# A two-layer hybrid encoder step: latent projections and their norm at head 0, norm crossings by pairs of tiles on the vector engine

## The reference

```python
h = rmsnorm(x, g_pre_mix)
(qn, qr, ckv, kr, qb, kb, vb, qc, kc, vc, alr, gc, gate) = split_cols(h @ w_in)
# A: latent attention, 8 heads: c = rmsnorm(ckv, g_kv); keys c @ w_uk, values c @ w_uv; rope on qr and kr
# B: sliding-window attention, 8 query heads on 2 key heads, window 128, sinks and ALiBi
# C: gated linear attention, 4 heads: loga = log_sigmoid(alr @ w_alpha + b_alpha) / 16,
#    a recurrence over tokens, then rmsnorm(o, g_gla) * silu(gc)
y = sigmoid(gate_a) * (oa @ w_up_a) + sigmoid(gate_b) * (ob @ w_up_b) + sigmoid(gate_c) * (oc @ w_up_c)
x = x + rmsnorm(y @ w_out, g_post_mix)
f = square(relu(rmsnorm(x, g_pre_mlp) @ w_ff1)) @ w_ff2          # d_ff = 4096
x = x + rmsnorm(f, g_post_mlp)
```

## Time and profile before

| | us |
|---|---|
| median of 3 runs | 2562.69 (2556.35, 2562.69, 2563.92) |
| profiled execution | 2563.45 |
| its span, first to last instruction | 2561.7 |
| PE busy | 2422.8 (95%) |
| PE weight loads (beside PE) | 2250.9 (88%) |
| POOL busy | 1139.4 (44%) |
| DVE busy | 1039.7 (41%) |
| ACT busy | 951.5 (37%) |
| mean granted TensorE clock | 0.974 |
| PE's share of the chain that ended last | 86% (DVE 8%, ACT 3%) |

### The profile page before, as it was taken

How to read it: one execution, slowest core, us unless ns; L and a number is a source line. 1 busy time by engine, 2 the same in 40 slices (tenths; PEclk the granted TensorE clock), 3 DMA queues, 4 the chain that set the end, 5 groups by cost and what they waited for, 6 DMA issues and landing times.

```text
span 2561.7 us, 42155 instructions
## 1 busy us (share of the span) xinstructions
PE 2422.8 (95%) x17852; PEld 2250.9 (88%) x17852; DVE 1039.7 (41%) x1884; ACT 951.5 (37%) x1835; POOL 1139.4 (44%) x733
## 2 busy tenths in 40 slices
PE   6899999999999799999979999999999997999997
PEld 5799987888789799999968999688987996999997
DVE  4545555543632621111365564455256227111114
ACT  3344333342345432322334443244334554423222
POOL 5433323443446555545444442144334565545443
PEclk9899999999999999999988999999999998999999
DMA  4111231112124022222211112211211231222222
GB/s 161 34 50 56 86 89 42 50 58 74 42 60 169 32 75 85 89 83 83 100 63 41 63 56 85 69 59 50 74 54 46 67 143 50 82 84 84 90 75 78
DMA packets 58940, 187.75 MB, mean 73 GB/s; under 512 B 7873, under 2 KB 16801, under 8 KB 58113
## 3 DMA queue, kind: packets, MB, share of 16 engines
q1 hardware_dynamic: 48608, 164.33, 20.4%
q10 hardware_dynamic: 10144, 20.73, 2.5%
HBM read 170.87 MB, written 10.89 MB: 71 GB/s over the span
## 4 chain that ended last, share of the span: by engine, by line
PE 86%; DVE 8%; ACT 3%; issue 1%; POOL 1%; DMA 0%; ACTq 0%; POOLq 0%; DVEq 0%; SPq 0%
PE dense L780 46%; PE att L780 21%; PE att L826 2%; PE att L1015 2%; PE att L1077 2%; DVE h_raw L1654 2%; PE att L964 1%; PE att L903 1%; PE att L889 1%; PE att L980 1%; DVE nsum L1607 1%; PE att L1049 1%; PE att L907 1%; PE att L1031 1%; DVE mix L1621 1%
## 5 line engine op out<-in xcount | busy, mean ns | idle before, releaser
L1995 POOL TENSOR_TENSOR wlo<-wraw,whi 128x1024 fp32r<-128x1024 f32 x302 | 731.8, 2429 | 881.9 <-ACT whi L1146 881.9
L780 PE MATMUL dense<-h_hi,whi 128*128 128x280 f32 (+1 forms) x2256 | 676.4, 300 | 20.1 <-POOL h_lo L2000 14.6
L780 PE MATMUL dense<-h_lo,whi 128*128 128x280 f32 (+1 forms) x2256 | 664.0, 294 | 0.0
L780 PE MATMUL dense<-h_hi,wlo 128*128 128x280 f32 (+1 forms) x2256 | 663.1, 294 | 0.0
L780 PEld LDWEIGHTS dense<-h_hi,whi 128*128 128x128 f32 (+1 forms) x2256 | 430.7, 191 | 46.4 <-ACT h_hi L1150 15.8
L780 PEld LDWEIGHTS dense<-h_hi,wlo 128*128 128x128 f32 (+1 forms) x2256 | 430.2, 191 | 1.8 <-issue 0.8
L780 PEld LDWEIGHTS dense<-h_lo,whi 128*128 128x128 f32 (+1 forms) x2256 | 430.2, 191 | 0.0
L1146 ACT ACTIVATE whi<-wraw 128x1024 fp32r<-128x1024 f32 x302 | 315.7, 1050 | 298.0 <-DMA wraw<-in_w 263.9
L780 PE MATMUL att<-h_hi,whi 128*128 128x280 f32 (+1 forms) x784 | 236.4, 301 | 20.4 <-POOL h_lo L2000 15.2
L780 PE MATMUL att<-h_hi,wlo 128*128 128x280 f32 (+1 forms) x784 | 233.6, 298 | 0.0
L780 PE MATMUL att<-h_lo,whi 128*128 128x280 f32 (+1 forms) x784 | 233.6, 298 | 0.0
(11 more groups left out here) (308 smaller groups left out, 4843.8 us busy)
## 6 DMA issues: line engine op xcount, KB each, us to landing
wraw<-in_w SPq DMA_DIRECT2D x302, 512.0 KB, 3.6
x_spill<-x ACTq DMA_DIRECT2D x2, 2240.0 KB, 7.2
x<-x_spill ACTq DMA_DIRECT2D x2, 2240.0 KB, 12.0
k_cat<-k_rope ACTq DMA_DIRECT2D x16, 212.0 KB, 3.5
x<-in_x SPq DMA_DIRECT2D x4, 560.0 KB, 6.1
out_y_out<-x SPq DMA_DIRECT2D x4, 560.0 KB, 3.1
out_c_out<-ckv ACTq DMA_DIRECT2D x2, 560.0 KB, 6.6
const<-in_const SPq DMA_DIRECT2D x1, 1112.0 KB, 12.1
```

What stands on the lines that cost most here:

```text
L780: mm = pe.matmul(bank(u, o, hf)[0:m, :], a[:, k, o * 128:o * 128 + m], b[:, k, H[hf]], start=(k == 0 and i == 0), stop=(k == kt - 1 and i ...
L1995: pool.tensor_tensor(wlo[slot][:, :], wraw[slot][:, :], whi[slot][:, :].bitcast(F32), ALU.subtract).then_inc(pool_done, st.done("pool", f" ...
```

## The change

1. The two ckv units come after cv 0 and cv 1 of head 0 instead of after head 3; both run before "p lev 0" of head 0. Their square and `prep_a` 0 (mean, rstd, scaling) move there too, with the mean in banks M_ and O_; ckv, kb and vb get places of their own at the end of SBUF.
2. The `prep_a` steps behind head 3 are dealt over six dense units instead of five; the loads of w_uk and w_uv move ahead by two units and those of the cached rows stay; kb and vb come in the last two attention steps of A, and `prep_b` 0 comes one unit behind attention A instead of two.
3. POOL clears k_rope at the new "load" step instead of before head 0's arguments, and amat and the zero state as soon as kralr is evacuated.
4. In a crossing, rstd stands first in the plan, ahead of the units' evacuations; the norm is dealt in four pairs of tiles between the units (two before the first, one before the second, one before the third). DVE adds pairs of x tiles in one instruction, ACT squares pairs, DVE adds the pairs (560 columns) and folds the two halves at the end. POOL has no part in it. All h_lo of tokens are DVE's, two tiles in one instruction for tiles 2 to 7.
5. Sums of the units' squares are added one unit later (`add_later`).
6. The squares of ff1 go from DVE to ACT.
7. During a crossing a "w" step is placed only if its unit begins within 5 halves.

```diff
-        units += [("cq", h), ("ck", h), ("cv", 2 * h), ("cv", 2 * h + 1), ("cg", 2 * h), ("cg", 2 * h + 1)]
-    units += [("ckv", 0), ("ckv", 1), ("qr", 0), ("qr", 1)] + [("qn", n) for n in range(4)]
+        units += [("cq", h), ("ck", h), ("cv", 2 * h), ("cv", 2 * h + 1)]
+        units += [("ckv", 0), ("ckv", 1)] if h == 0 else []
+        units += [("cg", 2 * h), ("cg", 2 * h + 1)]
+    units += [("qr", 0), ("qr", 1)] + [("qn", n) for n in range(4)]
...
-        cksq = at("cksq", [P, 2, T], F32, r_x)
+        cksq = at("cksq", [P, 2, T], F32, r_oc + 14 * row)
+        ckv_off = 229344 - 2 * row
+        assert wk["next"] <= ckv_off
+        ckv = at("ckv", [P, KL, T], F32, ckv_off)
...
+                    plan.append((l, ("rstd", post, hf)))
+                    norms = iter(range(4))
                     for i, u in enumerate(units):
+                        for j in (next(norms) for _ in range((2, 1, 1, 0, 0)[i])):
+                            plan.append((l, ("norm", post, hf, j)))
+                        if i == LAP - 2 and pre:
+                            plan.extend([(l, ("sums", pre, hf)), (l, ("rstd", pre, hf))])
                         plan.append((at_l, ("half", u, 1 - hf)))
                         if i == 0:
-                            plan.extend([(l, ("ms", post, hf)), (l, ("norm", post, hf))])
-                        if i == LAP - 2:
+                            plan.append((l, ("ms", post, hf)))
+                        if i == LAP - 2 and pre:
                             plan.extend([(l, ("ms", pre, hf)), (l, ("tokens", pre, hf))])
...
                         gla_steps((0, "v lev 0"), (0, "v arg 2"), (0, "v lev 1"), (0, "v end"), (0, "v lev 2"))
+                dense(2)
+                order.append(("prep_a", "square"))
                 gla_steps((0, "p lev 0"), (0, "v kend"), (0, "v amat 0"), (0, "v amat 1"), (0, "v amat 2"))
+                order.append(("prep_a", 0))
                 dense()
...
+                    if h + 1 == C_HEADS:
+                        order.append(("prep_a", "load"))
...
                 last = C_HEADS - 1
                 dense()
                 gla_steps((last, "p o"), (last, "v o"))
-                order.append(("prep_a", "load"))
+                order.append(("prep_a", "load cache"))
                 dense()
                 gla_steps((last, "p ms"), (last, "v rstd"))
-                order.append(("prep_a", "square"))
-                dense()
-                gla_steps((last, "v out"))
-                order.append(("prep_a", 0))
-                for steps in ((1, 2), (3, 4, 5), (10, 11), (6, 7), (8, 9, 12, 13)):
+                for steps in ((1, 2), (3, 4), (5, 10, 11), (6, 7, 8), (9, 12), (13,)):
                     dense()
-                    if steps[0] == 1:
+                    order.extend([("prep_a", s) for s in steps])
+                    if 1 in steps:
+                        gla_steps((last, "v out"))
+                    if 5 in steps:
                         gla_steps((last, "v oc"))
-                    order.extend([("prep_a", s) for s in steps])
                 for j in range(len(JOBS["a"]) + 2):
                     order.append(("att", "a", j))
                     dense()
-                dense(2)
+                dense()
                 order.append(("prep_b", 0))
                 dense(2)
                 order.append(("prep_b", 1))
-                dense(2)
+                dense()
                 for j in range(len(JOBS["b"]) + 2):
                     order.append(("att", "b", j))
                     dense()
...
+                    lap(l, "post_mlp", None, (l, U_MLP), (l, []))
+                    plan.append((l, ("ms", "post_mlp", 1)))
+                    plan.extend([(l, ("norm", "post_mlp", 1, j)) for j in range(4)])
...
+                if step[0] == "rstd" and l_ >= 0 and step[1:] in (("post_mix", 0), ("post_mlp", 0)):
+                    crossing = True
+                if step[0] == "tokens" and step[2] == 1:
+                    crossing = False
...
+                    if crossing and begun_at[key] - now > 5:
+                        break
...
+                    if s == 0:
+                        pe.wait_ge(act_done, A("act", "ckv sq"))
+                        for k in range(KL):
+                            for hf in range(2):
+                                mm = pe.matmul(ps[:, (M_, O_)[hf], 0:HALF], c_("ones_v"), cksq[:, k, H[hf]],
+                                               start=(k == 0), stop=(k == KL - 1))
+                        mm.then_inc(pe_done, st.done("pe", "prep a 0"))
...
+                        t = hid[g % 2][0][:, n % 8, c]
+                        act.wait_ge(act_done, A("act", f"evac {u} 0 {hfs[-1]}"))
+                        act.activation(t, t, ACT.Square).then_inc(act_done, st.done("act", f"hid {n}" + end))
...
+                def square_x(which, j, hf):
+
+                    if j == 0 and hf == 1:
+                        act.wait_ge(pe_done, A("pe", f"ms {which} 0"))
+                    if j >= 2:
+                        act.wait_ge(dve_done, A("dve", f"sum {which} {j - 1} {hf}"))
+                    dst = nsum[:, 1 if j == 0 else 3, :].rearrange("p (a n) -> p a n", a=2)
+                    act.activation(dst, x[:, 2 * j:2 * j + 2, H[hf]], ACT.Square).then_inc(act_done, st.done("act", f"sq {which} {j} {hf}"))
+
+                def norm(which, hf, j):
                     if which == "post_mlp" and l + 1 == DEPTH:
                         return
-
-                    def ready(k):
-                        e = x_engine(k)
-                        act.wait_ge(by_name[e], A(e, f"x {which} {k} {hf}"))
-
-                    square_x("pre_mlp" if which == "post_mix" else "next", hf, ready)
+                    act.wait_ge(dve_done, A("dve", f"x {which} {2 * j + 1} {hf}"))
+                    square_x("pre_mlp" if which == "post_mix" else "next", j, hf)
...
-                        act.wait_ge(pe_done, A("pe", f"gla o {C_HEADS - 1}"))
-                        for dst, name in ((wuk, "w_uk"), (cct, "a_ckv"), (wuv, "w_uv")):
+                        act.wait_ge(pe_done, A("pe", f"gla lev {C_HEADS - 1} 4"))
+                        for dst, name in ((wuk, "w_uk"), (wuv, "w_uv")):
                             act.dma_start(dst[:, :, :], io[name][bass.ds(l, 1)].rearrange("a (k p) n -> p (a k) n", p=P)
                                           ).then_inc(a_loaded[name], 16)
+                    if s == "load cache":
...
+                        for hf in range(2):
+                            link(act.activation(rstd[:, H[hf]], ps[:, (M_, O_)[hf], 0:HALF], ACT.Ln, bias=eps[:, 0:1]),
+                                 "prep a 0" if hf == 1 else None)
                         act.activation(rstd[:, :], rstd[:, :], ACT.Exp, scale=-0.5).then_inc(act_done, st.done("act", "c rstd"))
...
+                waiting = []
+
+                def add_waiting():
+                    while waiting:
+                        add_square(*waiting.pop())
+
+                def add_later(u, hf):
+                    add_waiting()
+                    waiting.append((u, hf))
...
+                def add_square_x(which, j, hf):
+
+                    dve.wait_ge(act_done, A("act", f"sq {which} {j} {hf}"))
+                    if j >= 2:
+                        dve.wait_ge(dve_done, A("dve", f"sum {which} {j - 1} {hf}"))
+                    if j >= 1:
+                        total = nsum[:, 1, :]
+                        dve.tensor_tensor(total, total, nsum[:, 3, :], ALU.add).then_inc(dve_done, st.done("dve", f"sum {which} {j} {hf}"))
+                    if j == 3:
+                        dve.wait_ge(dve_done, A("dve", f"sum {which} 3 {hf}"))
+                        dve.tensor_tensor(nsum[:, 1, 0:HALF], nsum[:, 1, 0:HALF], nsum[:, 1, HALF:T], ALU.add
+                                          ).then_inc(dve_done, st.done("dve", f"sum {which} 7 {hf}"))
...
+                    if j == 0:
+                        add_waiting()
+                        dve.wait_ge(act_done, A("act", f"rstd {which} {hf}"))
...
+                    for k in (2 * j, 2 * j + 1):
                         t = src[:, k, H[hf]]
                         dve.scalar_tensor_tensor(t, t, p_("g_" + which, k), rstd[:, H[hf]], ALU.mult, ALU.mult
                                                  ).then_inc(dve_done, st.done("dve", f"nrm {which} {k} {hf}"))
-                        if x_engine(k) == "dve":
-                            dve.wait_ge(dve_done, A("dve", f"nrm {which} {k} {hf}"))
-                            dve.tensor_tensor(x[:, k, H[hf]], x[:, k, H[hf]], t, ALU.add).then_inc(dve_done, st.done("dve", f"x {which} {k} {hf}"))
-                        if pre and k >= 3:
-                            add_square_x(pre, k - 2, hf)
-                    if pre:
-                        add_square_x(pre, KD - 2, hf)
-                        add_square_x(pre, KD - 1, hf)
+                    if pre and j >= 1:
```

(17 more changed lines are left out.)

167 lines of the change are left out of this document (56 added, 111 removed).

## The result

The changed kernel takes 2499.24 us (median of four runs, 2492.84 to 2505.84), the kernel before 2563.31 beside it: a ratio of 0.976, 95% interval 0.9741 to 0.9779. Forecast were 2500 us. The profiled execution took 2499.4 us, with a span of 2497.3 of which PE is busy for 2397.2 (before: 2422.8 of 2561.7). PE's own work is the same (17852 matmuls in both), so the 25.6 us less of busy time are work that had run at the lower clock level. The mean granted clock rose from 0.974 to 0.989.

A forecast was written before the change was run, and what follows sets the result against it. TensorE (PE), busy 2422.8 of 2561.7 us, was taken to bound the kernel, so only its lost time could be won. 23 + 12 + 11.5 + 7.5 + 8 - 3 + 2 + 2 = 63 off 2563.45 gave 2500; range 2482 to 2534.

The forecast's parts named there:

- Head 0: Both layers, before the level matmuls: two ckv units cut PE's loss to 6.5 us from 19.2 and 17.6; gain 23.
- Rival 2: Head 0: the split of weights bounds it, both ckv units' wlo 3 us later per layer; 2512 us, chance 0.14.
- Rival 5: Head 0: more gain comes, it runs without waits; 2487 us, chance 0.07.
- Mix crossings: Both layers: first half's tokens 1.7 us sooner, second half's earlier rstd cuts PE's 7.04 us wait to 3; gains 12 and 11.5.
- Squares of ff1 on ACT: 74 squares, some 50 us, moved from DVE to ACT: no effect, at worst 7 us.
- Mlp crossing: 1270 to 1325 us: first half gains 5, the second also gains; sum 7.5 us, between 2 and 14.
- Latent preparation: Six units cover the steps instead of five, a 1.7 us wait remains; gain 8 us for both layers, between 0 and 12.
- New small waits: Attention steps, each with another unit beside it: 3 us against the sum, from -3 to 8.
- Start 2 and end 2: Kernel start: h_lo sooner, gain 2 us (-2 to 4); end: last x sooner and a wait gone, gain 2 (0 to 3).
- Signs named in advance: Right if no wait over 4 us before level matmuls, mean-square waits near 20 us, second-half clock 1.00; wrong if paired adds over 1.
- Rival 1: Crossings and head 0: the clock falls anyway at every remaining gap, costing 28 us (18 in crossings); 2528 us, chance 0.14.
- Rival 3: Crossing halves: DVE alone is too slow, some 66 pieces each 1.8 us longer beside POOL; 2619 us, chance 0.04.

The follow-up runs named there:

- latent_back: Changed kernel with the ckv units, latent norm, preparation steps and POOL's k_rope zeroing back in their old places, crossings as changed: median 28 us higher.
- wide_banks: Changed kernel with ckv 0 and 1 weights loaded and split early, and four banks for these units' halves: median 10 us lower.
- rstd_late: Changed kernel with post-norm rstd and norm pieces back behind each lap's first half unit, weight-split deferral kept: median 6 us lower.
- out_later: Changed kernel with head 3's output steps (v out, v oc) one unit later in the preparation: by its median not distinguishable from the changed kernel.
- prep_new: Changed kernel with head 3's output steps two units later and the key copies of step 5 on ACT: median 10 us lower.
- no_defer: Changed kernel without the rule that puts off weight splits during a crossing: median 4 us higher.

## Why the prediction was right, step by step

- **Head 0** (23 forecast; 20.2 in the first trace, 25.7 in the second, 28 by latent_back with the preparation). In the first trace the waits came as read: 3.40 and 2.82 us for 3.3 and 3.2. That the level matmuls would run at full clock held, but ckv 1 did not: 0.50 between 75 and 80 us. In the second trace, the usual case, ckv 0 itself was slow and hid the second wait. The sum had 6.5 us of waits and no clock; both traces lost to the clock, and the usual one made up for it with the wait that it hid. Rival 2 had the right place (the split) and the wrong depth: with the split early, the bank behind the level products takes over with 4.92 us. Rival 5 needed both out of the way, and happened in wide_banks' layer 0.
- **Mix crossings** (12 and 11.5; measured 13.8 and 12.1). The chain took 10.1 us from the first nrm to the mean-square matmul for 10.4, the tokens 6.1 for 6.4. In the second half the wait was 2.23 for 3; the clock stayed at 1.00 in layer 0, not in layer 1. Layer 1 had not "the same rows": before the change its second half waited 4.69 us and not 7.04, and another 4.7 for an h_lo. The total was right, one of its causes wrong: I named rstd's new place first, and with the other two parts in place it is worth nothing (rstd_late). The squares on ACT and the deferral both carry it: in layer 0 the wait is 7 us again with either undone, in layer 1 it is 6.78 without the one and 4.24 without the other. Their prices of 4 to 6 us a crossing can hardly add, since one wait of 7 us is all there was; no run has both undone.
- **Squares of ff1 on ACT** (forecast: nothing, at worst 7) is the step that failed in its place: I looked at ACT's load only, and not at what leaves DVE's queue. The row was there: the square that took 2.20 us also waited 0.94 us for ACT. The runs put it at 11 us in the two mix crossings by the trace and 6 by the median. Its price sat in the crossing's sum, so the total did not suffer.
- **Mlp crossing** (7.5; measured 6.3). The wlo that "may still fall there" did, at 1250.09 us, beside an h_lo of 2.38 us.
- **Latent preparation** (8; measured 1.9 and 0.1, and 1.5 of the 1.9 is one unit behind head 3's wait that was slow before): the mis-sized term. The wait forecast at 1.7 us was 3.94, since v out took 5.3 us instead of 3.1 (one operation of 2.95 beside a wlo), and the unit behind it took 8.67 us instead of 6.5, a loss to the clock that the sum left out. That makes 6 us a layer, as much as before. And the step was wrong in kind: out_later removed v out from that place and the wait moved. Six units in place of five give DVE no less to do.
- **New small waits** (-3): there are none; attention gave 0.9 us by the waits alone, and -3.6 in the second trace, where the clock fell with no wait of PE in front (0.51 and 0.50 in the windows from 1895 to 1905 us; the unit at 1899.87 took 8.88 us instead of 6.4, the short matmuls ahead of it were slow too).
- **Start 2 and end 2**: 3.1 and 1.1.
- **Signs named in advance**: no wait before the level matmuls, paired adds all at 0.73 to 0.75 us and no new wait of attention above 3 us came as said. The waits before the mean-square matmuls did not: 28.3 us in all instead of "near 20". My own sum left 2.3 to 3 us of wait in a half, and the start's 15 us untouched, so that sign contradicted the sum that it stood beside.
- **Rival 1** (the clock falls anyway, 28 us) is half true. In both traces of the changed kernel it did fall behind the waits of head 0 and of the preparation, behind those of the heads in some places, and in the mix crossing of layer 1 (0.93 over it), but not in layer 0's. The Trainium skill ("TensorE: Matmul & The Clock Gate", the section on a second failure mode, cycling through PSUM banks) describes a clock that swings under brief, frequent idling. The trace agrees for head 0 and in part for layer 1's crossing, and disagrees for that of 828 to 890 us, where 1.00 stands beside waits of 1.89 and 2.23. The 18 us for the crossings were this rival's own price, and they did not come.

So the total was hit by three terms of nearly the right size (head 0, the mix and the mlp crossings: 54.8 us forecast, 52.4 in the first trace) and by errors that cancel: 6 too much in the preparation against 4 too little for small waits and 5 that the heads got by chance. That the median came out within 1 us of 2500 is luck in that sense: the mechanisms of head 0 and of the crossings' chains were right, but hardly to 1 us, and the second measurement was 2503. Rival 3 did not come about: the paired adds take 0.74 us.

## What to carry to other kernels

Moving filler work in front of a stalled engine only helps as far as the filler's own inputs come in time, and its bank's release is one of them: follow it to the queue that it stands in. Where an engine works through a stretch without a pause, a reordering may only move the wait (out_later); taking work from it and putting the rest behind what PE needs shortened it here (prep_new). When an operation is moved off an in-order queue, price what it waited for there, not only its duration, and take a second trace of the same kernel before giving a clock difference to an edit.

## What the runs showed of the hardware

The same wait of PE, 1.52 us, is followed by the same 48 matmuls in 5.29 or 7.88 us in two executions and layers of one kernel, and in 8.89 in the kernel before. By an estimate from the mean granted clocks, the changed kernel spent about 55 us at the lower clock in one execution and 85 in another. In the crossing of no_defer DVE and POOL slowed each other: a paired add of 0.74 us took 2.87, and the wlo beside it 2.83 instead of 2.39. In the changed kernel all 32 paired adds took 0.73 to 0.75 us for 560 columns.
